# A two-layer hybrid diffusion block on one core: semaphores cleared by SyncE in the following stage, one barrier at each seam, early weight tiles handed over first

## The reference

```python
for l in range(DEPTH):
    mod_l = jax.nn.silu(c) @ mod_w[l] + mod_b[l]
    mod_c = jax.nn.silu(c_ctx) @ mod_w[l] + mod_b[l]
    ...
    hl = _modulate(_rmsnorm(xl, norm1_g[l]), sh1, sc1)
    hc = _modulate(_rmsnorm(xc, norm1_g[l]), sh1c, sc1c)
    ...
    ym_l, ym_c = _mlstm_branch(...)
    ya_l, ya_c = _diff_branch(...)
    yh_l = _hyena_seq(...)
    mix_l = _merge(ym_l, ya_l, yh_l, pl[11], merge_b[l], w_br_m[l], w_br_a[l], w_br_h[l], w_out[l])
    ...
    xl = xl + g1 * mix_l
    tok = _modulate(_rmsnorm(xl, norm2_g[l]), sh2, sc2).reshape(B * L, D)
    ...
    f = _moe(tok, router_w, router_b, e_w1[l], e_w3[l], e_w2[l])
    xl = xl + g2 * f[:B * L].reshape(B, L, D)
return xl
```

## Time and profile before

| | |
|---|---|
| median of 3 runs | 3386.18 us (3379.64 to 3388.25) |
| the profiled execution: its own time | 3385.86 us |
| its span | 3384.1 us |
| TensorE busy | 3038.8 us, 90% |
| weight loads (beside TensorE) | 2553.1 us, 75% |
| VectorE busy | 2059.7 us, 61% |
| ScalarE busy | 1541.4 us, 46% |
| mean granted TensorE clock | 0.951 of full speed |
| HBM traffic | 187 GB/s over the span, 403 to 423 GB/s in the slices of the MoE stages |
| chain that ended last | back to 3352.28 us only |

### The profile page before, as it was taken

The page is one execution under the profiler, slowest core; times in us unless marked ns, Lnnn a source line. Parts: engine busy times, 40 slices in busy tenths (PEclk is TensorE's granted clock), DMA queues, the critical chain, the costliest instruction groups (busy, mean ns, idle before and its releaser), DMA issues. The chain is left out here.

```text
span 3384.1 us, 47102 instructions
## 1 busy us (share of the span) xinstructions
PE 3038.8 (90%) x16892; PEld 2553.1 (75%) x16892; DVE 2059.7 (61%) x3054; ACT 1541.4 (46%) x2269; POOL 0.2 (0%) x4
## 2 busy tenths in 40 slices
PE   8899899979998898799999978788779976999998
PEld 7687766657877777688888748766578875899997
DVE  2455745466455742487787656655465555888885
ACT  3322244533343231376767443334334444667764
POOL 0000000000000000000000000000000000000000
PEclk8999999989999998999999989999989998999999
DMA  5111411033121423599999403431062234999994
GB/s 200 56 68 75 165 59 53 25 143 125 63 75 62 174 107 149 212 407 407 403 405 406 173 38 112 181 121 56 25 236 87 76 126 156 410 421 423 423 422 167
DMA packets 77189, 634.05 MB, mean 187 GB/s; under 512 B 9806, under 2 KB 11792, under 8 KB 13328
## 3 DMA queue, kind: packets, MB, share of 16 engines
q1 hardware_dynamic: 77072, 632.51, 47.1%
HBM read 631.43 MB, written 1.05 MB: 187 GB/s over the span
## 5 line engine op out<-in xcount | busy, mean ns | idle before, releaser
L183 PE MATMUL ps<-rounded,rounded 128*128 128x256 f32 (+1 forms) x1856 | 643.1, 346 | 107.9 <-DVE rounded L174 62.6
L2530 DVE TENSOR_TENSOR rounded<-high_arena,rounded 128x1024 fp32r<-128x1024 f32 x512 | 592.3, 1219 | 165.6 <-ACT rounded L2474 165.6
L184 PE MATMUL ps<-rounded,rounded 128*128 128x256 f32 (+1 forms) x1856 | 631.5, 340 | 0.0
L185 PE MATMUL ps<-rounded,rounded 128*128 128x256 f32 (+1 forms) x1856 | 631.0, 340 | 0.0
L159 PEld LDWEIGHTS ps<-low_arena,high_arena 128*128 128x128 f32 x4672 | 536.1, 193 | 25.7 <-issue 13.6
L159 PE MATMUL ps<-low_arena,high_arena 128*128 128x128 f32 x4672 | 537.5, 276 | 19.2 <-DMA high_arena<-in_e_w 11.5
L174 DVE TENSOR_TENSOR rounded<-low_arena,rounded 128x1024 fp32r<-128x1024 f32 (+3 forms) x344 | 367.6, 1096 | 288.3 <-ACT rounded L170 284.4
L2474 ACT ACTIVATE rounded<-high_arena 128x1024 fp32r<-128x1024 f32 x512 | 498.8, 1049 | 17.6 <-PE ps L2434 14.6
L183 PEld LDWEIGHTS ps<-rounded,rounded 128*128 128x128 f32 x1856 | 363.7, 196 | 152.9 <-DVE rounded L174 79.8
L2433 PE MATMUL ps<-rounded,rounded 128*128 128x512 f32 x1024 | 420.1, 410 | 23.8 <-DVE rounded L2530 23.8
L170 ACT ACTIVATE rounded<-low_arena 128x1024 fp32r<-128x1024 f32 (+3 forms) x344 | 313.0, 949 | 212.0 <-PE ps L185 114.1
(11 more groups left out here) (320 smaller groups left out, 3145.0 us busy)
## 6 DMA issues: line engine op xcount, KB each, us to landing
high_arena<-in_e_w SPq DMA_DIRECT2D x248, 1024.0 KB, 8.1
high_arena<-in_e_w SPq DMA_DIRECT2D x77, 2048.0 KB, 10.0
low_arena<-in_d_wm SPq DMA_DIRECT2D x48, 1024.0 KB, 4.8
high_arena<-in_d_modlater SPq DMA_DIRECT2D x40, 1024.0 KB, 6.9
low_arena<-in_d_wml SPq DMA_DIRECT2D x32, 1024.0 KB, 4.9
low_arena<-in_d_wh SPq DMA_DIRECT2D x16, 1536.0 KB, 7.0
low_arena<-in_d_wa SPq DMA_DIRECT2D x16, 1536.0 KB, 6.6
low_arena<-in_d_wo SPq DMA_DIRECT2D x8, 1024.0 KB, 4.8
```

What stands on the lines that cost most here:

```text
L183: pe.matmul(out, l_hi, r_hi, start=(k == 0), stop=False)
L184: pe.matmul(out, l_lo, r_hi, start=False, stop=False)
L185: last = pe.matmul(out, l_hi, r_lo, start=False, stop=(k == n - 1))
L2530: v.tensor_tensor(w_lo[i % NB], pair_of(i), w_hi[i % NB].bitcast(F32), ALU.subtract).then_inc(w_split, 1)
```

## The change

The clears of a stage's semaphores are taken from the seam and put at the end of SyncE's program in the following stage; `stage` no longer makes a barrier of its own, so that the block's is the only one. The semaphores are given back one stage later, and the names get a parity, since two stages' semaphores now live at once. The clears of the last MoE stage stand in the result stage, behind the wait for the output; the result stage's own semaphore is not cleared. In the merge stages the two hand-overs are put ahead of the other transfers.

```diff
+LEFT, PARITY = [], [0]
+
+
 @contextmanager
 def stage(nc, *names):
 
-    sems = [nc.alloc_semaphore(name) for name in names]
+    PARITY[0] = 1 - PARITY[0]
+    sems = [nc.alloc_semaphore(f"{name}_{PARITY[0]}") for name in names]
     yield sems
-    for s in sems:
-        nc.sync.sem_clear(s)
-    nc.all_engine_barrier()
-    for s in sems:
+    for s in LEFT:
         nc.release_semaphore(s)
+    LEFT[:] = sems
+
+
+def clear_left(sp):
+
+    for s in LEFT:
+        sp.sem_clear(s)
...
@@ stage_merge @@
         def _(sp):
             def load(u, s):
                 sp.dma_start(*merge_tile(K, l, branch, u, s)).then_inc(tile_in[s], 16)
+            for s in range(2):
+                K.early.hand_over(sp, s, tile_in[s])
             if mod_tiles:
                 sp.dma_start(cond, K.A["d_cond"][:, streams[0]:, :]).then_inc(cond_in, 16)
                 for s in range(2):
...
             if branch == 1:
                 for dst, src in gate_consts(K, l):
                     K.early.issue(sp, 3, dst, src)
-            for s in range(2):
-                K.early.hand_over(sp, s, tile_in[s])
             for u in range(2, KC + 2):
...
+            clear_left(sp)
...
```

More of the change, by code:

```diff
@@ L2684, in _ @@
             sp.wait_ge(result_out, 16)
+            clear_left(sp)
 def build(nc, A):
     K = Core(A)
+    LEFT.clear()
     with ExitStack() as ctx:
```

## The result

| | before | after |
|---|---|---|
| median of the runs | 3386.34 us, 4 runs | 3361.77 us, 4 runs (3359.31 to 3362.78) |
| the profiled execution: its own time | 3385.86 us | 3362.78 us |
| its span | 3384.1 us | 3360.8 us |
| mean granted clock | 0.951 | 0.956 |

The ratio is 0.993 (95% interval 0.9917 to 0.9944): 24.6 us faster, where 35.4 were forecast. 3361.8 us lies 1.8 us above the range.

The account below looks back on a forecast made before the run. TensorE was busy nine tenths of the span, so only idle stretches could be given back. Seams 31.4 (after the end's clears), hand-overs 1.8 and clock 2.2 made 35.4 us off 3385.9: forecast 3351 us, range 3343 to 3360.

Parts of the forecast that it names:

- seams, with halts: At 19 seams between stages, clears 28.1 us, second barriers 4.75 and SyncE's halts within clears 2.4: 35.3 us.
- 61 clears behind the output: At the program's end, the MoE clears move from before the output to behind its landing: 3.9 us not saved.
- hand-overs and clock, all stages: Earlier hand-overs in merge stages give 1.8 us; TensorE's higher clock after shorter idle times at three seams gives 2.2 us.
- cover under SyncE's idle time: Moved clears cost nothing where SyncE finishes early; its smallest wait, last merge stage, is 8.7 us against 2.2 of clears.
- That fits by 0.8 us, so the whole 2.04 us is kept: Layer 0's branch-1 merge: the third tile's rounding ends before VectorE wants it, so the earlier start's 2.04 us lasts.
- For the other seams I count nothing: Beyond three named TensorE restarts, the clock was taken to bring no gain or loss; the clock term's bounds: 0 to 5.9 us.
- the three named stretches: TensorE restarts at granted 0.50: first mLSTM stage 3.3 us, second 5.2, last merge stage 3.3; costing 5.9 us in all.
- Rival A: TensorE's clock gives nothing or takes, and halts surface: 3355 us, or 3358 with two more slow stretches; chance 0.28.
- Rival C: Second barriers hid work such as code fetching, so part of every seam returns: 3360 to 3376 us, 0.07; no change, 0.03.
- D: Slower: a late second weight tile delays the condition and modulation transfers in merge stages; from 3396 us, chance 0.01.
- The two signs: Named as showing the forecast wrong: stalls over 0.5 us at a stage's head booked to nothing, or stages ending on SyncE.

Follow-up runs that it names:

- the filler run: Changed kernel plus two unread identity products behind the fourth mixing product, in the first three heads of layer 0's mLSTM stage: 3354.16 us.
- clears_under_output: Changed kernel with SyncE's 61 last clears put between the output's issue and the wait for its landing: 3357.65 us.

## Why the prediction was wrong

The sum of the prediction was 35.4 us; the two profiles differ by 23.3. By its steps:

| step | forecast | measured |
|---|---|---|
| seams, with halts | 35.3 | 35.2 |
| 61 clears behind the output | -3.9 | -3.2 |
| hand-overs and clock, all stages | 1.8 + 2.2 | -5.8 |
| stall outside all steps: the branch | 0 | -3.0 |

**Seams: right.** Size and cover under SyncE's idle time were as put. The halts still come, four of 0.4 us in the changed kernel, but in SyncE's idle time. The clears at the end were sized 0.7 too high, mostly since I took the 61 of the MoE seam with their halt.

**"That fits by 0.8 us, so the whole 2.04 us is kept" is the step that failed.** The mechanism was right, in the merge stage of the kernel before the 2.03 us are all there. I followed them to the next stall of that stage and stopped. The part alone made the kernel before no faster (1.9 us slower, by an interval that just takes in no change), and taking it out of the changed kernel gained 3.7 to 5.0 us. In the changed kernel even the merge stage kept only 0.9 us. There TensorE is at half clock from 731.8 to 735.2 (the first row), and VectorE later waits 1.34 us for it, where it waited 0.18 before; the difference is the 1.16 us that are missing:

```profile
731.80:735.20 3.40, 3.40 (x9) 2.64 (x8) 3.40 (x7) 0.00 (x0) 0.00 (x0) 0.50 1.03 434
```

```profile
744.45 0.69 DVE L1029 SCALAR_TENSOR_TENSOR high_arena<-high_arena,ps 128x512 f32<-128x512 f32 x1 [1.34 <-PE ps L193]
```

And before:

```profile
750.73 0.69 DVE L1018 SCALAR_TENSOR_TENSOR high_arena<-high_arena,ps 128x512 f32<-128x512 f32 x1 [0.18 <-PE ps L185]
```

**"For the other seams I count nothing" was the wrong bound for the clock.** Of the three named stretches two went and one half went, as put or better. But I bounded the term at 0 from below, as if a clock could only be regained at places where it had been lost. The two waits of 1.89 us in the mLSTM stage were at full clock before and are not in the changed kernel; that alone is 3.4 us, by the filler run. Rival A had the mechanism ("everything behind a seam now falls elsewhere against that chance") with a size of 3 us for two stretches; what it called chance is, for these stretches, fixed by the program, which is why it did not average out over the runs.

The second half of the error is that gains and losses did not weigh the same here. In merge 0 of layer 0 TensorE was busy 1.9 us less than before and the stage still took 0.6 us more: at its next wait for VectorE it stands for 6.60 instead of 4.07 us, and goes on 19.3 us after the stage's start in both (before, then after). Where the 0.6 us behind it come from was not taken apart.

```profile
1110.01 0.47 PE L183 MATMUL ps<-rounded,rounded 128*128 128x512 f32 x1 [4.07 <-DVE low_arena L1026]
```

```profile
1103.61 0.77 PE L191 MATMUL ps<-rounded,rounded 128*128 128x512 f32 x1 [6.60 <-DVE low_arena L1037]
```

Here and at the head of the mLSTM stage the regained clock was handed to the next wait; the falls in the middle of a long run of products were paid in full. This fits that TensorE's busy time stayed the same while the stages grew.

The Trainium skill (TensorE: Matmul & The Clock Gate, "HAM oscillation — how this bites in real kernels") warns of long idle gaps alone; by that rule short ones keep the higher clock. The rows do not agree with it as a rule on the gap's length alone: behind 1.89 us the clock stayed full in one program and fell in the other, and behind 2.10 us it was full at 806.3 and at half at 2507.7.

**Rival C was kept at the wrong price.** I had it as code fetched under the barriers at each seam. Of that there is nothing: at every seam the first computing instruction of TensorE, VectorE and ScalarE stands as far behind the release as before, to 0.05 us, or nearer. What there is is one branch, 3.0 us, in none of the prediction's terms, set by the number of instructions ahead of it and not by the time. My evidence against C, a table load behind an inner block, was from layer 0, where it holds to this day. D did not come up. The two signs that I had named for being wrong, a stall at a stage's head or a stage that ends on SyncE, did not come either; the loss lies in the middle of stages, where neither looks.

**Still open.** Why the same wait is followed by a fall at one moment and not at another; why the branch costs 3.4 us at one place in the code and 0.4 at another (no run tests what it waits for). And stages of layer 1 that gained and lost 2 to 3 us each were not taken apart: merge 2 (+3.4), norm and filter (-2.8) and attention (-2.4) did so in both profiles of each kernel, within 0.4 us. Merge 2 and attention belong together: in `clears_under_output`, whose program is the same up to there, they take 62.8 and 237.7 instead of 65.0 and 235.5 us, 300.5 in sum either way. So of the two only their sum, 1.0 us more than before, is a loss.

## What to carry to other kernels

Time taken out where all engines stand still was gained one for one, 35.2 us for 35.3; count the instructions and believe the sum. Time gained by one engine has to be followed through the stages behind it, and the edit measured alone and with the rest: here one that did in its own stage what it should, 2.0 us, cost 4.4 us in the next. And when a profile shows falls of TensorE's clock behind waits in the middle of its work, try to fill those waits with products that nobody reads, behind the last instruction that anybody waits for: it gave 3.4 us in one stage here, and one place too early it cost 3.6.

## What the runs showed of the hardware

- TensorE's falls to the lower clock in the mLSTM stage of layer 0 came at the same waits in five profiles (the changed kernel three times, and two runs whose edits lie in later stages), which gave it 279.8 us each time; 1.0 us of idle time ahead of the stage moved them away (276.4 us).
- One compare-and-branch on TensorE takes 3.36 to 3.86 us in six profiles and 0.37 to 0.47 us in eight, according to how many instructions stand ahead of it in the program; 27 to 48 more make it short, 6 do not. The median of the 22 branches is 0.21 us.
- A barrier of all engines costs 0.33 us where nothing else is going on (three in a row) and 0.37 us in the mean of the 19 at the seams; a semaphore clear on SyncE 0.055 us, and 0.057 us under a transfer in flight, which is not slowed by it (the result stage takes 5.24 us, and 5.25 before).
